# Three feed-forward layers: high weights meet high and low tokens in one 512-column up product, with ScalarE copying the low columns and VectorE adding the high ones

## The chip, the core and the metric

The program runs on one core of a Trainium2 chip. The metric is the device time in microseconds. The kernel before takes 1206.23 us, the median of three runs (1205.76, 1206.23 and 1207.28 us).

## What is computed

Two blocks follow each other on 256 tokens of width 1024. The first block is a gated linear attention mixer and a SwiGLU feed-forward layer (the FFN below). The second block has two layers, each a mixer and a squared-ReLU MLP. So there are three feed-forward layers:

```python
def swiglu(h, w_in, w_out):                 # the FFN: w_in 1024 x 5632, w_out 2816 x 1024
    gate, up = jnp.split(h @ w_in, 2, axis=-1)
    return (jax.nn.silu(gate) * up) @ w_out
...
for layer in range(DEPTH_2):                # two MLPs: mlp_w1 1024 x 4096, mlp_w2 4096 x 1024
    ...
    x = x + sq_relu_mlp(rms_norm_2(x, norm_mlp[layer]), mlp_w1[layer], mlp_w2[layer])
```

`sq_relu_mlp` squares the positive part of the up product, relu(xn @ w1)^2 @ w2. Everything is fp32.

## The kernel before

**Split products.** TensorE multiplies in the fp32r type, which keeps fewer bits than fp32. Each operand is therefore split in a high part, the value rounded to fp32r, and a low part, the rest. A product is three passes of TensorE that accumulate in one PSUM region (`split_mm`, L2105 to L2110): high by high (L2108), high by low (L2109) and low by high (L2110). The left factor of `split_mm` is the stationary one; it is loaded into the array before each pass, also where L2109 uses the same one as L2108. The high part of a weight tile is made by ScalarE (`high`, L687 to L690), the low part by VectorE (`low_weights`, L1169; it calls `low`, L1167).

**A feed-forward step.** The hidden width is worked off in steps: 128 gate and 128 up columns a step in the FFN (22 steps, numbered f = 0 to 21), 256 columns a step in an MLP (16 steps, twice). In one step of any of them the up product has 16 stationary weight tiles of 128x128 (8 tiles deep, times two halves: gate and up, or the two column halves). Each meets 256 tokens. The step's two halves land side by side in one PSUM bank, `bank[4 + j % 2]`. Then the hidden values are made and split:

- FFN: ScalarE writes silu(gate) from PSUM to `act_a` (L850). VectorE multiplies it with the up half in PSUM (L1473), casts the high part (L1474), and subtracts for the low part (L1167).
- MLP: ScalarE writes relu of both halves (512 columns) to `act_a` (L984). VectorE squares it (L1473), casts, subtracts.

The down product of the step has the hidden values as stationary operand and the down weights as moving one, 512 columns a pass: 12 passes in the FFN, 24 in an MLP, into banks 0 to 3.

**Order.** Each engine's queue is written out by hand, and semaphores tie them: `ff_ps` (up product done), `ff_act` (activation done), `ff_mid` (hidden values split), `w_used` (down product done), `loU_ready` and `loD_ready` (low part of the up and down weights ready), `hT_lo` (low part of the tokens ready, in four quarters). TensorE runs rounds of six steps in the FFN (rounds of four in an MLP): up(0), up(1), down(0), up(2), down(1), ..., up(5), down(4), down(5), then the next round. So within a round a down product has an up product between itself and the down product before it, and at a round's end two down products follow each other. The FFN's rounds end at f = 5, 11, 17 and 21. In each step ScalarE makes, after the activation, the high part of the up weights of two steps later and of the down weights of the next step, and VectorE makes the low parts after the hidden values. During the first round and a half of the FFN GpSimd sums slices of another weight matrix (`mod_sums`, L556 to L571).

## Time and profile before

| | |
|---|---|
| median of 3 runs | 1206.23 us |
| the profiled execution's own time | 1206.26 us |
| its span | 1204.5 us |
| TensorE busy | 1158.5 us (96%), 7472 matmuls |
| weight loads busy | 1005.1 us (83%) |
| VectorE busy | 741.7 us (62%), 1048 instructions |
| ScalarE busy | 556.6 us (46%), 760 instructions |
| GpSimd busy | 113.6 us (9%) |
| HBM traffic | 174 GB/s over the span |
| where they lie | FFN 233 to 421 us, MLPs 549 to 727 us and 1016 to 1195 us, about |

The busy time of an engine is the time in which at least one of its instructions is under way. Matmuls overlap: the duration of one is longer than the distance from its start to the next one's start. So what a pass costs is read from the starts, not from the durations. The ScalarE and VectorE rows give real durations. In a row of the timeline, brackets at the end hold the idle time before the instruction and what ended it.

### The profile page before, as it was taken

Reading aid. Unit: us, or ns where it says so; the run is one execution under the profiler, and the core shown is the slowest. Engines: PE = TensorE matmul, PEld = TensorE weight load, DVE = VectorE, ACT = ScalarE, POOL = GpSimd, SP = SyncE. Lnnn points to the kernel's source line nnn. Section 1 sums busy time; section 2 is a strip of 40 time slices with the busy share of each in tenths; the row PEclk is TensorE's granted clock in tenths of the full one; section 3 lists DMA queues with packets and bytes.
Section 4 is the critical chain, followed back from the end, with each engine's and each line's share of the span. In section 5 each row is a group of like instructions: output and inputs, shape, how many; then the busy total and the mean of one; then the engine's idle time right before and its main releaser. Section 6 shows DMA issues by size and latency. Waiting matters only on the chain.

```text
span 1204.5 us, 19086 instructions
## 1 busy us (share of the span) xinstructions
PE 1158.5 (96%) x7472; PEld 1005.1 (83%) x7476; DVE 741.7 (62%) x1048; ACT 556.6 (46%) x760; POOL 113.6 (9%) x109
## 2 busy tenths in 40 slices
PE   5899998899999989999999999999999999999997
PEld 2587775699999988648999999999999988999996
DVE  2887335697554586745465456776667776654653
ACT  3753232634333453644343346666666655433432
POOL 1000051187100070000000000000000000000000
PEclk9999999899999999999999999999999999999999
DMA  9674464977755540708554635555555434745500
GB/s 352 222 268 165 137 241 105 323 226 241 213 181 179 172 99 1 279 2 282 207 185 168 222 105 144 137 141 156 157 157 157 147 130 161 271 170 205 190 19 36
DMA packets 200241, 209.42 MB, mean 174 GB/s; under 512 B 6027, under 2 KB 167190, under 8 KB 199990
## 3 DMA queue, kind: packets, MB, share of 16 engines
q1 hardware_dynamic: 196480, 197.41, 51.3%
q0 software_dynamic: 2928, 9.02, 2.7%
q10 hardware_dynamic: 774, 2.17, 0.5%
q8 instruction: 40, 0.66, 0.2%
q14 instruction: 19, 0.16, 0.0%
HBM read 207.53 MB, written 2.01 MB: 174 GB/s over the span
## 4 chain that ended last, share of the span: by engine, by line
PE 90%; DVE 4%; ACT 2%; DMA 2%; issue 1%; ACTq 0%; DVEq 0%; SPq 0%
PE bank L2108 23%; PE bank L2110 23%; PE bank L2109 23%; PE bank L2378 2%; PE bank L1932 2%; PE bank L1934 2%; PE bank L1933 2%; PE bank L2505 1%; PE bank L2490 1%; PE bank L2481 1%; PE bank L2515 1%; DMA weight_pool<-in_gla_w_in_dram 1%; PE bank L1863 1%; DMA normed<-in_ctx_dram 1%; DMA weight_pool<-in_mod_w_dram 1%; PE bank L2361 1%
## 5 line engine op out<-in xcount | busy, mean ns | idle before, releaser
L2108 PE MATMUL bank<-hT_high,mlp_up_high 128*128 128x256 f32 x512 | 145.2, 284 | 0.9 <-DVE hT_low L1511 0.9
L2110 PE MATMUL bank<-hT_high,mlp_up_low 128*128 128x256 f32 x512 | 144.9, 283 | 0.0
L2109 PE MATMUL bank<-hT_low,mlp_up_high 128*128 128x256 f32 x512 | 144.9, 283 | 0.0
L2108 PE MATMUL bank<-od_w_high,hT_high 128*128 128x384 f32 x376 | 130.1, 346 | 0.0
L2110 PE MATMUL bank<-od_w_high,hT_low 128*128 128x384 f32 x376 | 126.1, 335 | 0.0
L2109 PE MATMUL bank<-od_w_low,hT_high 128*128 128x384 f32 x376 | 125.8, 334 | 0.0
L1167 DVE TENSOR_TENSOR mlp_down_low<-weight_pool,mlp_down_high 128x2048 fp32r<-128x2048 f32 x32 | 73.3, 2290 | 59.2 <-ACT mlp_down_high L690 59.2
L1167 DVE TENSOR_TENSOR od_w_low<-weight_pool,od_w_high 128x3072 fp32r<-128x3072 f32 x24 | 80.5, 3356 | 40.9 <-ACT od_w_high L690 40.9
L2108 PEld LDWEIGHTS bank<-hT_high,mlp_up_high 128*128 128x128 f32 x512 | 98.1, 192 | 2.8 <-issue 1.9
L2108 PE MATMUL bank<-hT_high,ffn_up_high 128*128 128x256 f32 x352 | 99.9, 284 | 0.0
L2108 PE MATMUL bank<-mlp_down_high,hidden_high 128*128 128x512 f32 x256 | 99.9, 390 | 0.0
L2109 PE MATMUL bank<-mlp_down_low,hidden_high 128*128 128x512 f32 x256 | 99.9, 390 | 0.0
L2110 PE MATMUL bank<-hT_high,ffn_up_low 128*128 128x256 f32 x352 | 99.6, 283 | 0.0
L2109 PE MATMUL bank<-hT_low,ffn_up_high 128*128 128x256 f32 x352 | 99.6, 283 | 0.0
L2110 PE MATMUL bank<-mlp_down_high,hidden_low 128*128 128x512 f32 x256 | 99.6, 389 | 0.0
L2109 PEld LDWEIGHTS bank<-hT_low,mlp_up_high 128*128 128x128 f32 x512 | 98.2, 192 | 0.9
L2110 PEld LDWEIGHTS bank<-hT_high,mlp_up_low 128*128 128x128 f32 x512 | 98.2, 192 | 0.0
L690 ACT ACTIVATE mlp_down_high<-weight_pool 128x2048 fp32r<-128x2048 f32 x32 | 61.2, 1912 | 71.0 <-PE bank L2110 71.0
L984 ACT ACTIVATE work<-bank 128x512 f32<-128x512 f32 x32 | 19.1, 598 | 137.6 <-PE bank L2110 137.6
L1473 DVE TENSOR_TENSOR work<-work 128x512 f32<-128x512 f32 x32 | 22.1, 690 | 89.4 <-ACT work L984 89.4
L1167 DVE TENSOR_TENSOR mlp_up_low<-weight_pool,mlp_up_high 128x2048 fp32r<-128x2048 f32 x32 | 73.2, 2289 | 2.6 <-ACT mlp_up_high L690 2.6
L2108 PEld LDWEIGHTS bank<-od_w_high,hT_high 128*128 128x128 f32 x376 | 70.6, 188 | 1.3 <-DVE od_w_low L1167 0.3
(367 smaller groups left out, 2697.7 us busy)
## 6 DMA issues: line engine op xcount, KB each, us to landing
weight_pool<-in_mlp_w_dram SPq DMA_DIRECT2D x64, 1024.0 KB, 7.8
weight_pool<-in_od_w_in_dram SPq DMA_DIRECT2D x72, 512.0 KB, 5.2
weight_pool<-in_ffn_w_in_dram SPq DMA_DIRECT2D x44, 512.0 KB, 5.7
weight_pool<-in_mod_w_dram SPq DMA_DIRECT2D x20, 1024.0 KB, 8.1
weight_pool<-in_gla_w_in_dram SPq DMA_DIRECT2D x12, 1024.0 KB, 8.3
weight_pool<-in_ffn_w_out_dram SPq DMA_DIRECT2D x22, 512.0 KB, 7.0
weight_pool<-in_gla_w_out_dram SPq DMA_DIRECT2D x2, 2048.0 KB, 14.2
normed<-in_mod_w_dram POOLq DMA_DIRECT2D x16, 256.0 KB, 5.1
```

The costliest lines, as they stand in the source:

```text
L690: act.activation(dst[:, :], pool[:, e.at + off:e.at + off + dst.shape[1]], ACT.Copy).then_inc(s[done], 1)
L984: act.activation(act_a[:, j % 2, :], bank[4 + j % 2][:, :], ACT.Relu).then_inc(s["ff_act"], 1)
L1167: dve.tensor_tensor(dst, whole, high.bitcast(F32), ALU.subtract).then_inc(s[done], 1)
L1473: chain(dve.tensor_tensor(whole, *product, ALU.mult))
L1863: ins = mm(slice_bank(i, 0)[lo:lo + 32, :], silc[:, k, :], slice_weights(i, k), start=(k < 4), stop=(k >= 4))
L1932: mm(out_, left[0], right[0], start=start, stop=False)
L1933: mm(out_, left[0], right[1], start=False, stop=False)
L1934: return mm(out_, left[1], right[0], start=False, stop=stop)
L2108: mm(out_, left[0], right[0], start=start, stop=False, **flag)
L2109: mm(out_, left[0], right[1], start=False, stop=False, **flag)
L2110: return mm(out_, left[1], right[0], start=False, stop=stop, **flag)
L2378: ins = mm(bank[b][:, :], oT[:, k, P * t:P * t + P], pv(e)[:, k % 4, 512 * (b % 2):512 * (b % 2) + 512], start=(k == 4), stop=(k == 3))
```

## The change

The tokens' high and low parts lie one after the other in `hT`, and a strided view of both, `hT_both[:, k]`, is 512 columns in two pieces of 256. The up product of a weight tile is now two passes in place of three: the high weights meet all 512 columns, and the low weights meet the 256 high ones, which accumulate on the first half. So a half of a step fills a whole PSUM bank: columns 0 to 255 hold high by high plus low by high, columns 256 to 511 hold high by low, and the two halves of the bank have still to be added. A step has two banks, and banks 4 to 7 serve two steps.

ScalarE copies the two low halves to `act_a` (`low_products`), and VectorE adds the high halves from PSUM (`sum_halves`). In the FFN ScalarE then waits for the first sum (`ff_sum`) and takes the silu of it in SBUF. In an MLP the relu is folded into VectorE's square. The first step of the FFN takes another order of its tiles and no longer starts with a pass that zeroes a bank; step 19 waits for columns that use banks 6 and 7.

```diff
+        hT_halves = over("hT_halves", "hT", 0, 4096)
+        hT2 = [view(hT_halves, 2048 * i, KD, SEQ) for i in range(2)]
+        hT_both = hT_halves[:, :].rearrange("p (w k t) -> p k w t", w=2, k=KD)
+        def up_bank(j, part):
+            return bank[4 + 2 * (j % 2) + part]
...
# ScalarE
+            def low_products(j):
+                for part in range(2):
+                    ins = act.activation(act_a[:, j % 2, 256 * part:256 * part + 256], up_bank(j, part)[:, 256:512], ACT.Copy)
+                ins.then_inc(s["ff_act"], 1)
...
-                act.activation(act_a[:, j % 2, 0:256], bank[4 + j % 2][:, 0:256], ACT.Silu).then_inc(s["ff_act"], 1)
+                low_products(j)
+                act.wait_ge(s["ff_sum"], f + 1)
+                act.activation(act_a[:, j % 2, 0:256], act_a[:, j % 2, 0:256], ACT.Silu).then_inc(s["ff_act"], 1)
...
-                    act.activation(act_a[:, j % 2, :], bank[4 + j % 2][:, :], ACT.Relu).then_inc(s["ff_act"], 1)
+                    low_products(j)
...
# VectorE
+            def sum_halves(j, part):
+                v = act_a[:, j % 2, 256 * part:256 * part + 256]
+                return dve.tensor_tensor(v, v, up_bank(j, part)[:, 0:256], ALU.add)
...
-                dve.wait_ge(s["ff_act"], f + 1)
+                dve.wait_ge(s["ff_act"], 2 * f + 1)
+                sum_halves(j, 0).then_inc(s["ff_sum"], 1)
+                chain(sum_halves(j, 1))
+                dve.wait_ge(s["ff_act"], 2 * f + 2)
...
-                split_hidden(j, 256, (act_a[:, j % 2, 0:256], bank[4 + j % 2][:, 256:512]))
+                split_hidden(j, 256, lambda whole: dve.tensor_tensor(whole, act_a[:, j % 2, 0:256], act_a[:, j % 2, 256:512], ALU.mult))
...
-                    split_hidden(j, 512, (act_a[:, j % 2, :], act_a[:, j % 2, :]))
+                    both_sums = act_a[:, j % 2, :]
+                    split_hidden(j, 512, lambda whole: dve.scalar_tensor_tensor(out=whole, in0=both_sums, scalar=0.0, in1=both_sums,
+                                                                                op0=ALU.max, op1=ALU.mult))
...
# TensorE
+            def up_mm(out_, w, k, n):
+                mm(out_[:, :], w[0], hT_both[:, k], start=(n == 0), stop=False, skip_group_check=True)
+                return mm(out_[:, 0:256], w[1], hT2[0][:, k, :], start=False, stop=(n == KD - 1), skip_group_check=True)
...
+                if isinstance(f, int) and f == FF_LOOPS * FF_RING + 1:
+                    pe.wait_ge(s["mod_cols"], 12)
-                    if first and n == 0 and g == 0:
-                        mm(bank[4][:, :], zero[:, 0:P], zero[:, :], start=True, stop=False, skip_group_check=True)
...
-                            ins = split_mm(bank[4 + j % 2][:, 256 * f:256 * f + 256],
-                                           both(mlU[j % 2], lambda x: x[:, 256 * k + P * f:256 * k + P * f + P]),
-                                           both(hT2, lambda x: x[:, k, :]), n == 0, n == KD - 1)
+                            ins = up_mm(up_bank(j, f), both(mlU[j % 2], lambda x: x[:, 256 * k + P * f:256 * k + P * f + P]), k, n)
```

The order on ScalarE at the first two FFN steps; `work` is where `act_a` lies. Before:

```order
L690 ACTIVATE ffn_up_high<-weight_pool 128x2048 [waits w_ffn1,out_used]
L850 ACT_TABLE_LOAD
L850 ACTIVATE work<-bank 128x256 [waits ff_ps]
L690 ACTIVATE ffn_up_high<-weight_pool 128x2048 [waits w_ffn2]
L690 ACTIVATE ffn_down_high<-weight_pool 128x1024 [waits w_ffn1]
L850 ACTIVATE work<-bank 128x256 [waits ff_ps]
```

Now:

```order
L697 ACTIVATE ffn_up_high<-weight_pool 128x2048 [waits w_ffn1,out_used]
L856 ACTIVATE work<-bank 128x256 [waits ff_ps]
L856 ACTIVATE work<-bank 128x256
L865 ACT_TABLE_LOAD
L865 ACTIVATE work<-work 128x256 [waits ff_sum]
L697 ACTIVATE ffn_up_high<-weight_pool 128x2048 [waits w_ffn2]
L697 ACTIVATE ffn_down_high<-weight_pool 128x1024 [waits w_ffn1]
L856 ACTIVATE work<-bank 128x256 [waits ff_ps]
```

The silu, which stood first and waited for TensorE alone, now stands behind two copies and waits for VectorE's first sum; the weight parts behind it stand where they stood. The load of silu's table moved behind the copies of the first step.

VectorE from the second up weights' low part to the second step. Before:

```order
L1167 TENSOR_TENSOR ffn_up_low<-weight_pool,ffn_up_high 128x2048 [waits hiU_ready]
L1473 TENSOR_TENSOR work<-work,bank 128x256 [waits ff_act]
L1474 CAST hidden_high<-work 128x256 [waits dve_chain]
L1167 TENSOR_TENSOR hidden_low<-work,hidden_high 128x256 [waits dve_chain]
L1167 TENSOR_TENSOR ffn_up_low<-weight_pool,ffn_up_high 128x2048 [waits hiU_ready]
L1167 TENSOR_TENSOR ffn_down_low<-weight_pool,ffn_down_high 128x1024 [waits hiD_ready]
L1473 TENSOR_TENSOR work<-work,bank 128x256 [waits ff_act]
```

Now:

```order
L1182 TENSOR_TENSOR ffn_up_low<-weight_pool,ffn_up_high 128x2048 [waits hiU_ready]
L1488 TENSOR_TENSOR work<-work,bank 128x256 [waits ff_act]
L1488 TENSOR_TENSOR work<-work,bank 128x256
L1504 TENSOR_TENSOR work<-work 128x256 [waits ff_act,dve_chain]
L1494 CAST hidden_high<-work 128x256 [waits dve_chain]
L1182 TENSOR_TENSOR hidden_low<-work,hidden_high 128x256 [waits dve_chain]
L1182 TENSOR_TENSOR ffn_up_low<-weight_pool,ffn_up_high 128x2048 [waits hiU_ready]
L1182 TENSOR_TENSOR ffn_down_low<-weight_pool,ffn_down_high 128x1024 [waits hiD_ready]
L1488 TENSOR_TENSOR work<-work,bank 128x256 [waits ff_act]
```

Two additions that read PSUM came in ahead of the product, and the product itself now reads two operands in SBUF (`work<-work`), where it read one in PSUM (`work<-work,bank`).

TensorE at the start of the FFN's second round, up(6). Before:

```order
L2108 MATMUL bank<-hT_high,ffn_up_high 128x256 [waits hT_lo,ff_mid]
L2109 MATMUL bank<-hT_low,ffn_up_high 128x256
L2110 MATMUL bank<-hT_high,ffn_up_low 128x256
L2108 MATMUL bank<-hT_high,ffn_up_high 128x256
L2109 MATMUL bank<-hT_low,ffn_up_high 128x256
```

Now:

```order
L2184 MATMUL bank<-hT_halves,ffn_up_high 128x512 [waits hT_lo,ff_mid]
L2185 MATMUL bank<-hT_halves,ffn_up_low 128x256
L2184 MATMUL bank<-hT_halves,ffn_up_high 128x512
L2185 MATMUL bank<-hT_halves,ffn_up_low 128x256
L2184 MATMUL bank<-hT_halves,ffn_up_high 128x512 [waits hT_lo]
```

Three passes of 256 columns with three loads became one of 512 and one of 256 with two loads; the waits are the same.

## Rows read from the trace of the kernel before

**Rows 1.** the page: the chain that ended last, its shares by engine
```profile
PE 90%; DVE 4%; ACT 2%; DMA 2%; issue 1%; ACTq 0%; DVEq 0%; SPq 0%
```

**Rows 2.** windows, 300 to 350 us: busy us of each engine (instructions), granted clock, DMA share, GB/s
```profile
300.00:350.00 50.00, 50.00 (x354) 47.08 (x353) 29.39 (x31) 18.80 (x18) 6.14 (x4) 1.00 0.63 191
```

**Rows 3.** timeline, TensorE, a feed-forward step of the MLP: start us, duration us
```profile
599.79 0.28 PE L2108 MATMUL bank<-hT_high,mlp_up_high 128*128 128x256 f32 x1
...
605.55 0.40 PE L2108 MATMUL bank<-mlp_down_high,hidden_high 128*128 128x512 f32 x1
...
607.17 0.39 PE L2109 MATMUL bank<-mlp_down_low,hidden_high 128*128 128x512 f32 x1
...
611.02 0.28 PE L2108 MATMUL bank<-hT_high,mlp_up_high 128*128 128x256 f32 x1
...
611.25 0.28 PE L2110 MATMUL bank<-hT_high,mlp_up_low 128*128 128x256 f32 x1
```

**Rows 4.** timeline, TensorE, odd mixer's projection: 384 columns in three pieces
```profile
765.88 0.33 PE L2108 MATMUL bank<-od_w_high,hT_high 128*128 128x384 f32 x1
...
766.75 0.34 PE L2110 MATMUL bank<-od_w_high,hT_low 128*128 128x384 f32 x1
```

**Rows 5.** groups by form: busy us, mean ns of one, idle before
```profile
L2108 PE MATMUL bank<-hT_high,mlp_up_high 128*128 128x256 f32 x512 | 145.2, 284 | 0.9 <-DVE hT_low L1511 0.9
...
L2108 PE MATMUL bank<-hT_high,ffn_up_high 128*128 128x256 f32 x352 | 99.9, 284 | 0.0
...
L1551 DVE TENSOR_TENSOR work<-work 128x256 f32<-128x256 f32 x48 | 20.4, 425 | 1.6
```

**Rows 6.** timeline, ScalarE, end of the FFN
```profile
416.55 0.38 ACT L850 ACTIVATE work<-bank 128x256 f32<-128x256 f32 x1 [4.69 <-PE bank L2110]
416.83 1.59 ACT L690 ACTIVATE ev_c_high<-weight_pool 128x1664 fp32r<-128x1664 f32 x1
```

**Rows 7.** timeline, VectorE, end of the FFN
```profile
416.97 0.42 DVE L1473 TENSOR_TENSOR work<-work,bank 128x256 f32<-128x256 f32 x1 [3.85 <-ACT work L850]
417.43 0.29 DVE L1474 CAST hidden_high<-work 128x256 fp32r<-128x256 f32 x1
417.75 0.43 DVE L1167 TENSOR_TENSOR hidden_low<-work,hidden_high 128x256 fp32r<-128x256 f32 x1
```

**Rows 8.** timeline, TensorE, one down product of the FFN, and the next up product
```profile
304.10 0.40 PE L2108 MATMUL bank<-ffn_down_high,hidden_high 128*128 128x512 f32 x1
...
306.85 0.28 PE L2108 MATMUL bank<-hT_high,ffn_up_high 128*128 128x256 f32 x1
```

**Rows 9.** timeline, ScalarE, silu of the FFN's first and ninth step
```profile
239.06 0.38 ACT L850 ACTIVATE work<-bank 128x256 f32<-128x256 f32 x1 [2.60 <-PE bank L2110]
...
304.30 0.38 ACT L850 ACTIVATE work<-bank 128x256 f32<-128x256 f32 x1 [4.69 <-PE bank L2110]
```

**Rows 10.** timeline, VectorE, first round of the FFN: start, duration, idle before
```profile
236.27 2.28 DVE L1167 TENSOR_TENSOR ffn_up_low<-weight_pool,ffn_up_high 128x2048 fp32r<-128x2048 f32 x1
...
254.62 0.41 DVE L1473 TENSOR_TENSOR work<-work,bank 128x256 f32<-128x256 f32 x1
...
255.79 1.47 DVE L1167 TENSOR_TENSOR hidden_low<-work,hidden_high 128x256 fp32r<-128x256 f32 x1
...
262.24 0.42 DVE L1473 TENSOR_TENSOR work<-work,bank 128x256 f32<-128x256 f32 x1 [0.79 <-ACT work L850]
...
270.74 0.42 DVE L1473 TENSOR_TENSOR work<-work,bank 128x256 f32<-128x256 f32 x1 [1.47 <-ACT work L850]
...
279.24 0.42 DVE L1473 TENSOR_TENSOR work<-work,bank 128x256 f32<-128x256 f32 x1 [2.47 <-ACT work L850]
```

**Rows 11.** timeline, GpSimd in the same stretch
```profile
255.69 1.29 POOL L571 TENSOR_TENSOR normed<-normed 128x512 f32<-128x512 f32 x1
```

**Rows 12.** timeline, ScalarE, end of the first MLP
```profile
717.91 0.60 ACT L984 ACTIVATE work<-bank 128x512 f32<-128x512 f32 x1 [3.84 <-PE bank L2110]
```

**Rows 13.** timeline, VectorE, end of the first MLP
```profile
718.54 0.69 DVE L1473 TENSOR_TENSOR work<-work 128x512 f32<-128x512 f32 x1 [2.14 <-ACT work L984]
```

More of the change, by code:

```diff
@@ L1489, in _ @@
             with dve.Fori(0, FF_LOOPS - 1) as i:
-                chain.enter(i, 2 * FF_RING)
+                chain.enter(i, 3 * FF_RING)
                 for j in range(FF_RING):
@@ L2171, in ffn_up @@
                         pe.wait_ge(s["hT_lo"], n // 2 + 1)
-                    if first and n == 0 and g == 0:
-                        mm(bank[4][:, :], zero[:, 0:P], zero[:, :], start=True, stop=False, skip_group_check=True)
-                    ins = split_mm(bank[4 + j % 2][:, 256 * g:256 * g + 256],
-                                   both(ffU[j % 2], lambda x: x[:, 1024 * g + P * k:1024 * g + P * k + P]),
-                                   both(hT2, lambda x: x[:, k, :]), n == 0 and not first, n == KD - 1, running=first)
+                    ins = up_mm(up_bank(j, g), both(ffU[j % 2], lambda x: x[:, 1024 * g + P * k:1024 * g + P * k + P]), k, n)
                 ins.then_inc(s["ff_ps"], 1)
```

16 lines of the change are left out of this document (9 added, 7 removed).

## The prediction

> **What bounds the kernel now.** I read the chain of waits first. TensorE holds 90% of it [rows 1]: what shortens TensorE's own work in a feed-forward layer shortens the kernel, and work on the other engines counts only where TensorE comes to wait for it. The windows say the same of a stretch inside the FFN: TensorE is busy in 50.00 of 50 us, VectorE in 29.39 and ScalarE in 18.80, at a granted clock of 1.00, which is the 2.4 GHz level [rows 2].
>
> Then the timeline of TensorE, because the durations mislead. A 256-column pass has a mean duration of 284 ns [rows 5], but the 48 passes of one up product start between 599.79 and 605.55, so one costs 5.76 / 48 = 0.120 us. The down product behind it runs to 611.02; its last 17 passes, from 607.17 on, take 3.85 us or 0.2265 us each [rows 3]. The odd mixer's 384-column passes start 0.87 us apart over five, 0.174 us each [rows 4]. At 2.4 GHz the columns alone are 0.1067, 0.2133 and 0.160 us. Each size leaves the same remainder, 0.0133 us (0.014 for 384): what a pass costs is its columns plus about 13.3 ns, whatever their number, with one weight load a pass.
>
> **The passes, the gain.** The change leaves the number of columns as it is, 768 for a weight tile, and takes one pass and one load away: 3 x 0.120 = 0.360 us becomes 0.2267 + 0.120 = 0.3467 us. There are 352 tiles in the FFN and 512 in the MLPs [rows 5], 864 together, so 864 x 0.0133 = 11.5 us. I take this value. The moving operand now lies in two pieces; rows 4 has three pieces at the same remainder, so I cost this at nothing.
>
> No row shows 512 and 256 columns in turn for long, so the bounds come from where the two sizes meet. The first seven 512-column passes after a row of 256-column ones take 605.55 to 607.17, 1.62 us, against 7 x 0.2265 = 1.585; and the first two 256-column passes afterwards take 0.23 us, against 0.24 [rows 3]. So a change of sizes up costs about 0.03 us spread over some passes, and one down gives 0.01 back. The best case is that an alternating stream keeps what it gains: 13.3 + 1.7 ns, 13 us together. The worst is that every tile pays the 20 ns of a full round trip, which is a loss of 6.7 ns, -5.8 us together. In between, each 512-column pass is at 0.234 and each 256-column one at 0.120: 6 ns a tile, 5.2 us. I stay at 13.3, since a shift of a few ns in the start of a pass that is given back by the next is what the 0.01 looks like.
>
> The Trainium skill ("TensorE: Matmul & The Clock Gate", "Wait — 56ns, not 53.3ns?") puts the fixed cost of a warm pass at about 2.5 ns, and its "Step-by-step: what each phase is for" says that the next tile's weights load behind the running matmul; by these two, 864 passes fewer would be worth only 2.2 us. Rows 3 and 4 have 13.3 ns over the columns at three sizes, so here the trace disagrees, and the sum goes by the trace.
>
> **The hidden values, where nothing is lost.** Inside a round, TensorE has a down and an up product between the end of up(f) and down(f), 2.75 [rows 8] + 16 x 0.3467 = 8.3 us in the FFN. Even in an MLP at a round's end there is the whole down product, 605.55 to 611.02 = 5.47 us [rows 3]. In an MLP the relu of 0.60 us [rows 12] becomes two copies of 256 columns, 0.28 + 0.38 = 0.66 us [rows 6], then two additions of 0.42 [rows 7], then the square at 0.69 [rows 13], and cast and low part as before. I put the new square, which takes a maximum too, at the same 0.69; the chain grows by some 1.0 us and was about 2.7 us with its cast and low part (which I estimate from the FFN's at twice the columns). 3.7 us fit into 5.47, so both MLPs lose nothing; with additions twice as slow they still fit. VectorE's added 0.9 us a step are idle time now, in MLP and FFN alike (20 of 50 us in rows 2).
>
> The first step of the FFN loses its zeroing pass. That gains nothing: up(1) needs the low part of the second weights, which is ready at 236.27 + 2.28 = 238.55 [rows 10], and the first silu at 239.06, 0.2 us after up(0)'s end [rows 9], says that up(1) started at 238.86. Between them lie 0.3 us, which the 16 shorter tiles already use up. The silu's table load, now behind the copies, falls into the 5.5 us of up(1). Step 19's new wait on the mod columns stands a whole up product after they are asked for: nothing.
>
> **The hidden values at a round's end in the FFN, the loss.** Here only one down product of 2.75 us [rows 8] stands before down(f), at f = 5, 11, 17 and 21. The silu starts 0.20 us after that down product (304.30 against 304.10) [rows 8, 9]. At the end of the FFN this gives a down product from 416.35 to 419.10, and the low part was ready at 417.75 + 0.43 = 418.18 [rows 7]: 0.9 us to spare. Now, on the same time scale: copies 416.55 and 416.83, done 417.21; first sum 417.25 to 417.67; silu from SBUF at the same 0.38, 417.71 to 418.09, with the second sum beside it; product 418.13; cast 0.46 later, low part another 0.32 later and 0.43 long, done 419.34 [rows 6, 7]. That is 0.24 us too late, and with the release of TensorE about 0.4 us. Three round ends without GpSimd at work, f = 11, 17, 21: 1.2 us.
>
> The end at f = 5 is worse. While GpSimd runs [rows 11], VectorE's operations with two SBUF operands stretch: hidden_low of 256 columns took 1.47 us [rows 10], against 0.43 when alone [rows 7]. VectorE was behind in the first steps (no idle time before the product at 254.62), and from 262.24 to 279.24 it caught up, with 0.79, 1.47 and 2.47 us of idle time before its products [rows 10], 4.7 us in all. The change adds 0.9 us to each of about five steps and shortens each by 0.21, 5.6 us together, so that it has no spare time left and comes about 1 us late to f = 5. With the 0.4 us of the chain I take 1.5 us. The bounds are 0.4 (no lag) and 4 (each product stretched to 1.4 us as well, over three or four steps). The product that read PSUM kept 0.41 and 0.42 us in this stretch [rows 10], and it now reads two SBUF operands (the sibling with two SBUF operands takes 425 ns alone [rows 5]). The Trainium skill ("SBUF — State Buffer", "The single rule") says why that matters: the pair of ports that VectorE and GpSimd share is an exclusive lock, taken by a VectorE operation with two SBUF inputs. The 1.47 us beside GpSimd's 1.29 us operation at 255.69 [rows 11] agree.
>
> **The sum.** Made against the profiled execution: 1206.26 us, of which the span is 1204.5; this execution stands 0.03 us over the median. 1206.26 - 11.5 + 1.2 + 1.5 = 1197.5 us.
>
> **The rivals.**
> Size changes cost more than a load: 20 ns a tile, as in the round trip of rows 3. Then -13.3 turns to +6.7 ns, and with the 2.7 us of the round ends the time is 1206.3 + 5.8 + 2.7 = 1214.8. It decides from 13.3 ns a switch on. For it speaks that rows 3 do have a transient; against it that it dies out within seven passes of the same size and is given back in part. Chance 0.08.
> Half of it: 0.234 and 0.120, 1206.3 - 5.2 + 2.7 = 1203.8, on the edge of what can be told. Chance 0.08.
> The load is hidden and the 13.3 ns belong to each 256 columns written rather than to a pass: nothing is gained by the merge, and the 2.7 us of loss put the time at 1208.9; if the pass itself still frees some of it, it is less. Three equal remainders at three sizes [rows 3, 4] speak against it. Chance 0.05, on the edge between same and slower. With the 2.5 ns of the Trainium skill ("TensorE: Matmul & The Clock Gate", section named above) it would be 1206.8.
> VectorE falls behind further in the first round, the 4 us of the bound, and the other round ends cost 0.8 instead of 0.4 us: 1206.3 - 11.5 + 4 + 2.4 = 1201.2. The ports speak for it, and against it that GpSimd is busy for only 6.14 us after 300 us [rows 2], f = 8. Chance 0.10.
> More gain: 15 ns a tile and round ends that fit after all: 1206.3 - 13 + 0.6 = 1193.9. Chance 0.07.
> The rest, 0.62, is the forecast, 1195 to 1200.5.
>
> **Range and chances.** A measurement of this kernel can tell about 0.2%, 2.4 us, from no change; so faster means under 1203.8. Faster: forecast, more gain, the slow VectorE, and half of the half case: 0.83. Same: the other half and most of the 0.05 of the hidden load, 0.08. Slower: 0.09, with the rest of it. The range runs from 1194.0 to 1203.5: it leaves out most of the gain's case and the two bad ones.
>
> **What would show it.** Starts of TensorE inside an up product: a pair of 512 and 256 columns every 0.347 us right, 0.354 half, 0.367 wrong. The MLP step, 11.2 us in before (48 x 0.120 and 5.47), at 11.0. The idle time of TensorE before down(11), down(17) and down(21) at 0.4 us each, with VectorE's hidden_low as releaser, and 1 to 2 us before down(5); none before any down product of an MLP. VectorE's product in the first round at more than 0.42 us in places. The forecast is wrong if the pair takes over 0.354 us, or if TensorE waits inside rounds.

## The result, and the profile after

| | before | after |
|---|---|---|
| median of 14 runs each, us | 1206.39 | 1209.11 |
| lowest to highest, us | 1205.64 to 1207.64 | 1206.77 to 1212.16 |
| profiled execution: time, span, us | 1206.26, 1204.5 | 1208.3, 1206.5 |
| TensorE, first product of the FFN to that of the first MLP, us | 316.20 | 322.06 |
| first MLP's first product to the second's, us | 466.67 | 464.92 |
| second MLP's first product to the last pass, us | 179.42 | 177.63 |

The ratio is 1.0021 (95% interval 1.0013 to 1.0029): slower by 0.2%, where 1197.5 us and a gain were forecast. The last three lines, read from TensorE's timelines, say where. Both MLPs gained, 1.75 and 1.79 us, close to 16 steps x 0.112 us = 1.79. The FFN lost 5.86 us. The first of these lines runs on beyond the last down product, to the first MLP. All accounts below are those of the profiled execution, which is 0.8 us under the median; the times of after scatter over 5.4 us, those of before over 2.0.

The page's first and fourth parts, of the kernel after:

```profile
PE 1156.9 (96%) x6611; PEld 960.3 (80%) x6611; DVE 783.7 (65%) x1156; ACT 572.3 (47%) x836; POOL 110.3 (9%) x109
...
PE 72%; DVE 3%; ACT 1%; issue 0%; DVEq 0%; ACTq 0%
```

TensorE's share of the chain went from 90 to 72% [rows 1]. The busy shares hardly tell anything; the stretch of the FFN does.

Groups by line, of after (busy us, mean ns of one, idle before):

```profile
L2184 PE MATMUL bank<-hT_halves,mlp_up_high 128*128 128x512 f32 x512 | 181.9, 398 | 0.9 <-DVE hT_halves L1534 0.9
L2185 PE MATMUL bank<-hT_halves,mlp_up_low 128*128 128x256 f32 x512 | 143.7, 281 | 0.0
```

As in [rows 5] the mean duration misleads, and the starts count. Timeline of TensorE, after, one up product of the first MLP (start us, duration us):

```profile
599.39 0.40 PE L2184 MATMUL bank<-hT_halves,mlp_up_high 128*128 128x512 f32 x1
599.62 0.28 PE L2185 MATMUL bank<-hT_halves,mlp_up_low 128*128 128x256 f32 x1
599.74 0.40 PE L2184 MATMUL bank<-hT_halves,mlp_up_high 128*128 128x512 f32 x1
599.98 0.28 PE L2185 MATMUL bank<-hT_halves,mlp_up_low 128*128 128x256 f32 x1
600.10 0.40 PE L2184 MATMUL bank<-hT_halves,mlp_up_high 128*128 128x512 f32 x1
```

Unrounded, the starts stand 227, 113 and then 233, 117, 241, 120, 236, 113 ns apart, and these six come again and again: three pairs in 1060 ns, 353.3 a pair. With its start the whole up product takes 5.640 us for 16 pairs, 352.5 ns each (before 5.752 us), not 346.7. Against the 359.5 of before (5.752 / 16) that is 7.0 ns a tile, and 54 steps x 0.112 = 6.05 us in all instead of 11.5.

Not every stretch is like this. The second step of the same MLP has the same instructions in the same order:

```profile
560.37 0.39 PE L2184 MATMUL bank<-hT_halves,mlp_up_high 128*128 128x512 f32 x1
560.60 0.28 PE L2185 MATMUL bank<-hT_halves,mlp_up_low 128*128 128x256 f32 x1
560.71 0.39 PE L2184 MATMUL bank<-hT_halves,mlp_up_high 128*128 128x512 f32 x1
```

Here the starts stand 230 and 117 ns apart all the way, 346.7 ns a pair, and the up product takes 5.546 us: the number of the prediction. After runs at this pace in the FFN's first two steps (234.3 to 244.0) and around the second step of both MLPs (557.6 to 565.6 and 1022.5 to 1030.5), and at the slower one in nearly all the rest.

The FFN's first round, windows of after (busy us of TensorE, its loads, VectorE, ScalarE, GpSimd, then granted clock, DMA share, GB/s):

```profile
232.00:256.00 24.00, 23.20 (x119) 19.34 (x119) 21.12 (x22) 12.49 (x17) 16.61 (x14) 0.96 0.70 211
256.00:279.00 23.00, 23.00 (x123) 19.37 (x122) 22.17 (x22) 10.83 (x13) 15.80 (x15) 1.00 0.77 246
279.00:291.00 12.00, 8.48 (x34) 6.63 (x34) 10.82 (x9) 3.82 (x5) 9.03 (x7) 0.86 0.81 267
```

and of before:

```profile
256.00:279.00 23.00, 23.00 (x171) 21.98 (x170) 17.99 (x13) 7.75 (x8) 16.45 (x15) 1.00 0.87 276
279.00:291.00 12.00, 12.00 (x82) 11.09 (x81) 6.96 (x6) 3.94 (x5) 10.82 (x10) 1.00 0.78 234
```

VectorE had 5.0 us to spare between 256 and 279 us and has 0.8 now. Then TensorE is busy in only 8.48 of 12 us, at a mean clock of 0.86. Its timeline there, down(5):

```profile
281.82 0.39 PE L2137 MATMUL bank<-ffn_down_high,hidden_low 128*128 128x512 f32 x1
285.73 0.80 PE L2135 MATMUL bank<-ffn_down_high,hidden_high 128*128 128x512 f32 x1 [3.52 <-DVE hidden_low L1182]
286.32 0.63 PE L2136 MATMUL bank<-ffn_down_low,hidden_high 128*128 128x512 f32 x1
286.75 0.63 PE L2137 MATMUL bank<-ffn_down_high,hidden_low 128*128 128x512 f32 x1
...
288.45 0.49 PE L2135 MATMUL bank<-ffn_down_high,hidden_high 128*128 128x512 f32 x1
288.78 0.39 PE L2136 MATMUL bank<-ffn_down_low,hidden_high 128*128 128x512 f32 x1
```

Two passes start 3.91 us apart that should start 0.23 apart: a wait of 3.68 us. Behind it the passes start 0.427 us apart instead of 0.227, up to 288.5: the granted clock is at 1.2 GHz from 285.2 to 288.6. With the slow restart of the first passes that costs another 1.46 us.

Why VectorE was late, its timeline in after (the products and what surrounds them; idle before in brackets):

```profile
239.70 0.75 DVE L1488 TENSOR_TENSOR work<-work,bank 128x256 f32<-128x256 f32 x2 [1.44 <-ACT work L856]
241.50 1.27 DVE L1504 TENSOR_TENSOR work<-work 128x256 f32<-128x256 f32 x1 [1.04 <-ACT work L865]
...
243.13 1.59 DVE L1182 TENSOR_TENSOR hidden_low<-work,hidden_high 128x256 fp32r<-128x256 f32 x1
244.64 3.37 DVE L1182 TENSOR_TENSOR ffn_up_low<-weight_pool,ffn_up_high 128x2048 fp32r<-128x2048 f32 x1
247.94 2.06 DVE L1182 TENSOR_TENSOR ffn_down_low<-weight_pool,ffn_down_high 128x1024 fp32r<-128x1024 f32 x1
249.92 0.74 DVE L1488 TENSOR_TENSOR work<-work,bank 128x256 f32<-128x256 f32 x2
...
259.14 1.27 DVE L1494 CAST hidden_high<-work 128x256 fp32r<-128x256 f32 x1
...
282.25 0.74 DVE L1488 TENSOR_TENSOR work<-work,bank 128x256 f32<-128x256 f32 x2
283.19 0.54 DVE L1504 TENSOR_TENSOR work<-work 128x256 f32<-128x256 f32 x1 [0.21 <-DVE work L1488]
283.76 0.29 DVE L1494 CAST hidden_high<-work 128x256 fp32r<-128x256 f32 x1
284.09 1.58 DVE L1182 TENSOR_TENSOR hidden_low<-work,hidden_high 128x256 fp32r<-128x256 f32 x1
```

and ScalarE's, after:

```profile
244.56 0.66 ACT L856 ACTIVATE work<-bank 128x256 f32<-128x256 f32 x2 [0.41 <-PE bank L2185]
250.36 0.42 ACT L865 ACTIVATE work<-work 128x256 f32<-128x256 f32 x1 [5.14 <-DVE work L1488]
...
279.50 0.66 ACT L856 ACTIVATE work<-bank 128x256 f32<-128x256 f32 x2 [1.69 <-PE bank L2185]
```

In step 0 the copies end and the additions follow at once. In step 1 the copies are done at 245.22 and the additions start at 249.92, a lag of 4.7 us: the four stretched operations of the rows between took 1.27, 1.59, 3.37 and 2.06 us, where the same four take 0.43, 0.42, 2.31 and 1.22 us without GpSimd (run e3_gpsimd_idle), 3.9 us more. A lag of 1.3 us is there at this place in that run too, behind the table load of step 0, and is gone one step later. From step to step the lag is then 4.7, 3.1, 3.2, 2.4 and 2.1 us: it is being paid back, since VectorE needs 8.1 us a step (249.92 to 282.25 over four) and TensorE 8.4, but too slowly. Inside the round a down and an up product hide it. Before down(5) nothing does, and the wait is the sum of known parts: lag 2.1, hidden_low 1.58 instead of 0.43, product 0.54 instead of 0.42, and the 0.36 of a round end without GpSimd: 3.7 us.

The FFN's account: the passes give 22 x 0.112 = 2.46 us, the stretch is 5.86 us longer, so 8.3 us are lost. Down(5): 3.68 + 1.46 (clock and slow restart) = 5.1. Down(11), (17) and (21): 0.47 to 0.49 each, 1.4. Small new waits, each with its slow restart, before down(0) 0.5, up(2) 0.6 and up(3) 0.2: 1.3. The rest is 0.5. Some 0.3 of it lies in up(0) and up(1), which take 6.35 and, without the wait, 5.55 us (6.08 and 5.76 before): the clock was at half until 234.0 us, 1.6 us after the first product instead of 0.3. The other 0.2 has no place of its own; no run was made for this rest.

### The profile page after: what moved, and what is told of

Same layout as the page of the kernel before. It is cut to its first block, busy times and chain, and to the rows that moved or that the text cites. A ratio compares the mean times of both kernels' runs of the same rounds, so it can differ in the third digit from the quotient of the medians.

```text
span 1206.5 us, 17623 instructions
## 1 busy us (share of the span) xinstructions
PE 1156.9 (96%) x6611; PEld 960.3 (80%) x6611; DVE 783.7 (65%) x1156; ACT 572.3 (47%) x836; POOL 110.3 (9%) x109
## 4 chain that ended last, share of the span: by engine, by line
PE 72%; DVE 3%; ACT 1%; issue 0%; DVEq 0%; ACTq 0%
PE bank L2184 15%; PE bank L2135 13%; PE bank L2137 13%; PE bank L2136 13%; PE bank L2185 8%; PE bank L2409 2%; PE bank L2534 1%; PE bank L2519 1%; PE bank L2510 1%; PE bank L2544 1%; PE bank L2392 1%; PE bank L2148 1%; PE bank L2369 1%; PE bank L2525 1%; PE bank L2379 1%; PE bank L1877 0%
## 5 line engine op out<-in xcount | busy, mean ns | idle before, releaser
L2184 PE MATMUL bank<-hT_halves,mlp_up_high 128*128 128x512 f32 x512 | 181.9, 398 | 0.9 <-DVE hT_halves L1534 0.9
L2185 PE MATMUL bank<-hT_halves,mlp_up_low 128*128 128x256 f32 x512 | 143.7, 281 | 0.0
L2135 PE MATMUL bank<-od_w_high,hT_halves 128*128 128x384 f32 x376 | 130.1, 346 | 0.0
L2184 PE MATMUL bank<-hT_halves,ffn_up_high 128*128 128x512 f32 x352 | 125.9, 400 | 0.5 <-DVE ffn_up_low L1182 0.3
L2137 PE MATMUL bank<-od_w_high,hT_halves 128*128 128x384 f32 x376 | 126.1, 335 | 0.0
L2136 PE MATMUL bank<-od_w_low,hT_halves 128*128 128x384 f32 x376 | 125.8, 335 | 0.0
L2184 PEld LDWEIGHTS bank<-hT_halves,mlp_up_high 128*128 128x128 f32 x512 | 96.1, 188 | 25.6 <-issue 1.9
L2185 PE MATMUL bank<-hT_halves,ffn_up_low 128*128 128x256 f32 x352 | 99.1, 281 | 0.0
L2185 PEld LDWEIGHTS bank<-hT_halves,mlp_up_low 128*128 128x128 f32 x512 | 96.7, 189 | 0.9
L2135 PEld LDWEIGHTS bank<-od_w_high,hT_halves 128*128 128x128 f32 x376 | 70.6, 188 | 1.3 <-DVE od_w_low L1182 0.3
L2136 PEld LDWEIGHTS bank<-od_w_low,hT_halves 128*128 128x128 f32 x376 | 70.7, 188 | 0.0
L2137 PEld LDWEIGHTS bank<-od_w_high,hT_halves 128*128 128x128 f32 x376 | 70.5, 188 | 0.0
```

Of the source, the lines that this page charges most:

```text
L2135: mm(out_, left[0], right[0], start=start, stop=False, **flag)
L2136: mm(out_, left[0], right[1], start=False, stop=False, **flag)
L2137: return mm(out_, left[1], right[0], start=False, stop=stop, **flag)
L2184: mm(out_[:, :], w[0], hT_both[:, k], start=(n == 0), stop=False, skip_group_check=True)
L2185: return mm(out_[:, 0:256], w[1], hT2[0][:, k, :], start=False, stop=(n == KD - 1), skip_group_check=True)
```

## Experiments

Each result is set against runs of the kernel before on the same chip in the same stretch (medians 1206.31 to 1206.56). The three stretches of the profiled executions, us:

| run | median us | ratio (95%) | FFN | MLP to MLP | to the end |
|---|---|---|---|---|---|
| before | | 1 | 316.20 | 466.67 | 179.42 |
| after | 1209.11 | 1.0021 (1.0013 to 1.0029) | 322.06 | 464.92 | 177.63 |
| e1_mlp_only | 1202.45 | 0.9968 (0.9956 to 0.9980) | 315.84 | 464.89 | 177.63 |
| e2_grouped | 1207.78 | 1.0007 (0.9998 to 1.0017) | 323.34 | 464.50 | 177.23 |
| e3_gpsimd_idle | 1202.92 | 0.9973 (0.9963 to 0.9982) | 315.50 | 465.10 | 177.81 |
| e4_sum_in_bank | 1207.97 | 1.0009 (1.0000 to 1.0019) | 322.44 | 465.10 | 177.81 |
| e5_mlp_only_grouped | 1203.12 | 0.9970 (0.9957 to 0.9982) | 317.92 | 464.51 | 177.20 |
| e6_groups_of_two | 1206.64 (one) | none | 322.98 | 463.54 | 176.29 |
| e9_no_adds | 1200.81 | 0.9950 (0.9935 to 0.9965) | 313.76 | 464.91 | 177.81 |
| e10_continuous | 1204.54 | 0.9986 (0.9977 to 0.9996) | 316.91 | 464.90 | 177.64 |
| e11_continuous_twos | 1199.29 | 0.9935 (0.9918 to 0.9951) | 316.54 | 463.55 | 176.30 |
| e12_mlp_only_twos | 1200.30 | 0.9948 (0.9932 to 0.9965) | 315.87 | 463.58 | 176.28 |
| e13_paced_continuous_twos | 1196.97 | 0.9920 (0.9903 to 0.9936) | 312.87 | 463.55 | 176.28 |
| e14_paced | 1202.71 | 0.9966 (0.9954 to 0.9979) | 315.74 | 464.90 | 177.81 |

**e1_mlp_only.** The FFN as before, both MLPs as in after.

```diff
-                low_products(j)
-                act.wait_ge(s["ff_sum"], f + 1)
-                act.activation(act_a[:, j % 2, 0:256], act_a[:, j % 2, 0:256], ACT.Silu)
+                act.activation(act_a[:, j % 2, 0:256], bank[4 + j % 2][:, 0:256], ACT.Silu)
...
-                sum_halves(j, 0).then_inc(s["ff_sum"], 1)
-                chain(sum_halves(j, 1))
...
-                    ins = up_mm(up_bank(j, g), ...)
+                    ins = split_mm(bank[4 + j % 2][:, 256 * g:256 * g + 256], ...)
```

> The FFN as in the kernel before, the two MLPs with the merged up product. If the loss lies in the FFN's first round alone (theory), the MLPs keep what their 32 up products show in the trace of after, 5.64 instead of 5.752 us each: 32 x 0.112 = 3.6 us less than before, 1202.8 us, and no wait of TensorE before any down product. Rival, that something of the loss is spread over all three layers (a longer start of the MLPs, a lower clock): 1204.5 us or more.

Measured 1202.45 us. TensorE waits before no down product of an MLP, and its up products take 5.640 us there and 5.752 in the FFN. So the loss of after is in the FFN alone, 6.7 us between the two kernels (of which the profiles' FFN stretches show 6.2).

**e3_gpsimd_idle.** After, with GpSimd's products and additions on 8 of their 512 columns.

```diff
-g.tensor_tensor(w if k else sum_row(i), w, factor, ALU.mult)
+n8 = 8 if k else 512
+g.tensor_tensor((w if k else sum_row(i))[:, 0:n8], w[:, 0:n8], silc[:, k, 0:1].to_broadcast([P, n8]), ALU.mult)
...
-g.tensor_tensor(sum_row(i), sum_row(i), w, ALU.add)
+g.tensor_tensor(sum_row(i)[:, 0:8], sum_row(i)[:, 0:8], w[:, 0:8], ALU.add)
```

> The changed kernel, in which GpSimd's products and additions during the FFN's first round work on 8 of 512 columns (so the sums of two slices of the modulation weights are left out; its DMAs and signals stay). Theory, that VectorE is slowed by sharing its ports with GpSimd: VectorE's step in the first round falls from 8.3 us to about 6.4, TensorE's wait before down(5) from 3.5 to 0.4 us, the clock does not drop behind it, the waits before down(0) and up(2) go: 6 to 7 us less than after, about 1202.5 us. Rival, that the new chain (two copies, sum, silu, product) is what makes VectorE late: a wait of 3 us before down(5) stays, 1208 us or more.

Measured 1202.92 us. VectorE's timeline at the first round's end, e3_gpsimd_idle:

```profile
279.14 0.75 DVE L1489 TENSOR_TENSOR work<-work,bank 128x256 f32<-128x256 f32 x2 [2.24 <-ACT work L857]
280.10 0.43 DVE L1505 TENSOR_TENSOR work<-work 128x256 f32<-128x256 f32 x1 [0.21 <-DVE work L1489]
280.56 0.29 DVE L1495 CAST hidden_high<-work 128x256 fp32r<-128x256 f32 x1
280.89 0.43 DVE L1183 TENSOR_TENSOR hidden_low<-work,hidden_high 128x256 fp32r<-128x256 f32 x1
```

VectorE is idle for 2.24 us before the additions, nothing is stretched, and the two passes around the wait before down(5) start 0.601 us apart, a wait of 0.37. No clock drop, no wait before down(0) or up(2). GpSimd's load on VectorE is worth 6.2 us to this kernel, of which down(5) is 3.3 for the wait and 1.4 for the clock.

**e9_no_adds.** After, but silu and product read the banks directly; the part of gate and up that comes of high weights and low tokens stays out of the hidden values.

```diff
-                low_products(j)
-                act.wait_ge(s["ff_sum"], f + 1)
-                act.activation(act_a[:, j % 2, 0:256], act_a[:, j % 2, 0:256], ACT.Silu)
+                act.activation(act_a[:, j % 2, 0:256], up_bank(j, 0)[:, 0:256], ACT.Silu)
...
-                sum_halves(j, 0).then_inc(s["ff_sum"], 1)
-                chain(sum_halves(j, 1))
```

> The merged up product in all three layers, but in the FFN no copies and no additions: silu and product read the banks directly as before (so the high-by-low part of the FFN's gate and up values is left out), while GpSimd works as in the kernel before. Theory, that VectorE's and ScalarE's added work in the first round is what turns into TensorE's waits: no wait before down(0) to down(5) nor at later round ends, 54 x 0.112 = 6.0 us less than before, 1200.4 us. Rival, that the faster TensorE alone overtakes VectorE beside GpSimd: waits of 1 us or more before down(5) stay.

Measured 1200.81 us, and no wait before any down product. The FFN stretch is 313.76 us; 316.20 - 2.46 = 313.74. So TensorE's side of the change in the FFN is worth its passes and nothing else, and what after loses hangs on the copies and additions and on the silu's and product's wait for them.

**e4_sum_in_bank.** The second sum stays in PSUM, so that the product reads one operand there, as before.

```diff
-return dve.tensor_tensor(v, v, up_bank(j, part)[:, 0:256], ALU.add)
+v, b = act_a[:, j % 2, 256 * part:256 * part + 256], up_bank(j, part)[:, 0:256]
+return dve.tensor_tensor(b if in_bank else v, v, b, ALU.add)
...
+chain(sum_halves(j, 1, in_bank=True))
...
-... act_a[:, j % 2, 0:256], act_a[:, j % 2, 256:512], ALU.mult))
+... act_a[:, j % 2, 0:256], up_bank(j, 1)[:, 0:256], ALU.mult))
```

> The changed kernel, with VectorE's second addition in the FFN written back to the PSUM bank, so that the product reads one operand in PSUM as before. Theory, that the product's second SBUF operand let GpSimd's lock in: the product keeps 0.42 us in all six steps of the first round (in after up to 1.27, 1.1 us in all), VectorE is 1.1 us earlier at f = 5, and so is the end of TensorE's wait, about 1208 us. Rival, that the stretching moves on to the cast and hidden_low behind it: the product at 0.42, the wait before down(5) at 3.5 us as it was, 1209.1 us.

Measured 1207.97 us. VectorE's timeline, e4_sum_in_bank:

```profile
249.59 0.42 DVE L1504 TENSOR_TENSOR work<-work,bank 128x256 f32<-128x256 f32 x1 [0.21 <-ACT work L865]
250.05 1.09 DVE L1494 CAST hidden_high<-work 128x256 fp32r<-128x256 f32 x1
...
282.09 0.42 DVE L1504 TENSOR_TENSOR work<-work,bank 128x256 f32<-128x256 f32 x1 [0.20 <-DVE bank L1488]
282.54 0.29 DVE L1494 CAST hidden_high<-work 128x256 fp32r<-128x256 f32 x1
282.87 1.70 DVE L1182 TENSOR_TENSOR hidden_low<-work,hidden_high 128x256 fp32r<-128x256 f32 x1
```

The product takes 0.42 us in all six steps, but in each one the operation behind it takes the stretch: the cast 1.09 or 1.10 in three, hidden_low 1.15 to 1.70 in the others. The wait before down(5) is 4.0 us (passes 4.25 apart). The time agreed with the number that I gave my theory (but the 1.1 us to after lie within the scatter of both), the trace with the rival: what the product gains is lost one operation later, so the product's second SBUF operand isn't the cause.

**e10_continuous.** Down(5), (11) and (17) stand behind the next round's first up product.

```diff
                 for j in range(n):
                     ffn_up(f0 + j, j)
-                    if j:
-                        ffn_down(f0 + (j - 1), j - 1)
-                ffn_down(f0 + (n - 1), n - 1, last)
+                    if j or not first:
+                        ffn_down(f0 + (j - 1), (j - 1) % FF_RING)
...
+            ffn_down(FFC - 1, (FFC - 1) % FF_RING, True)
```

> The changed kernel, with TensorE's order in the FFN changed at the round ends: down(5), down(11) and down(17) stand behind the next round's first up product, like every other down product. Theory, that a lag of VectorE of some 3.5 us matters only where one down product of 2.75 us covers the hidden values: with 8.4 us of cover the wait before down(5), the clock's drop behind it (1.8 us) and the two 0.47 us waits go, up to 1 us comes back at the columns of step 18, about 1203.5 us. Rival, that VectorE beside GpSimd is too slow at every step: the wait only moves to the next products, 1206 us or more.

Measured 1204.54 us (1203.26 to 1206.52). No long wait and no clock drop are left; the waits at round ends are gone but for the last. Now TensorE meets the late VectorE in small pieces, 0.1 to 0.35 us before each of the seven up products that stand behind a down product from 246.6 to 298.9 us: it has caught up with it. Another 0.6 us come at 393.4, before the up product of step 19, where after has no wait of TensorE. The FFN takes 316.91 us, 0.7 more than before. Cover at the round end is worth 5.2 us of the FFN stretch; VectorE's load still costs the passes' gain.

**e14_paced.** After, with GpSimd's units spread: each waits until TensorE has used one more weight chunk.

```diff
                     g.wait_ge(s[f"sums_in{n % 2}"], 16 * (n // 2) + 16)
+                    if n:
+                        g.wait_ge(s["w_used"], n)
```

> The changed kernel with nothing but GpSimd paced, one unit a step. If the wait of 3.7 us before down(5) and the clock's drop behind it come from the density of GpSimd's work: a wait of 0.4 us there as at the other round ends, no drop, about 6 us less than the changed kernel and close to the run with GpSimd idle (1202.9): 1203.3 us. Rival, that any GpSimd work in a step costs VectorE the same: the wait stays at 2 us or more and comes at the later round ends too, 1208 us or more.

Measured 1202.71 us, 6.4 less than after for a wait on an engine that nothing waits for. Windows, e14_paced:

```profile
232.00:256.00 24.00, 23.33 (x124) 19.38 (x123) 20.64 (x29) 14.55 (x20) 6.71 (x7) 1.00 0.72 219
256.00:279.00 23.00, 23.00 (x124) 19.70 (x123) 18.70 (x17) 9.93 (x14) 14.47 (x9) 1.00 0.73 228
279.00:291.00 12.00, 11.79 (x61) 9.67 (x60) 7.14 (x8) 4.07 (x6) 7.78 (x6) 1.00 0.73 227
```

GpSimd is busy for 6.7 instead of 16.6 us up to 256, and VectorE, which has done 29 operations there instead of 22, comes out of the first steps without a lag. The wait before down(5) is 0.37 us, as at the other round ends (0.36), and the clock stays up. GpSimd still does all of its work.

**e2_grouped.** After, but in each half of an up product the eight 512-column passes stand first and the eight 256-column ones behind them (the FFN's first step as in after).

```diff
+            def up_group(out_, weights, ns, before=lambda n: None):
+                for n in ns:
+                    before(n)
+                    mm(out_[:, :], weights(K_ORDER[n])[0], hT_both[:, K_ORDER[n]], ...)
+                for n in ns:
+                    ins = mm(out_[:, 0:256], weights(K_ORDER[n])[1], hT2[0][:, K_ORDER[n], :], ...)
```

> The changed kernel with the same passes in another order: in each half of a step first the 8 passes of 512 columns, then the 8 of 256 (all steps but the FFN's first). Theory, that the missing 6 ns a pair are the price of changing the size: the up product takes 16 x 0.3467 plus one transient, 5.57 us instead of 5.64, and the kernel 53 x 0.07 = 3.7 us less than after, 1205.4 us. Rival, that a 512-column pass whose moving operand lies in two pieces costs 240 ns by itself: up product at 5.64 us, kernel at 1209.1 us.

Measured 1207.78 us. The up product takes 5.559 us, 347.4 ns a pair against the 346.7 that I had worked out for a pass with its load at 13.3 ns over its columns: the gain that I predicted is there in every step inside a round of an MLP when passes of one size stand together. Two things took it back. The wait before down(5) was 4.0 us, with 6.8 us at half clock behind it. And the first step of each MLP lost 1.0 us, TensorE's timeline, e2_grouped:

```profile
555.87 3.00 PE L2191 MATMUL bank<-hT_halves,mlp_up_high 128*128 128x512 f32 x8 [0.55 <-DVE hT_halves L1534]
558.70 1.12 PE L2193 MATMUL bank<-hT_halves,mlp_up_low 128*128 128x256 f32 x8
```

Eight 512-column passes take 2.83 us here and not 1.81, because hT's low parts arrive in pairs and the 256-column passes, which need none, no longer fill the time.

**e5_mlp_only_grouped.** e1 with the groups of e2 in the MLPs.

```diff
-                    ins = up_mm(up_bank(j, f), ...)
+                    for n0 in range(0, KD, 8):
+                        ins = up_group(up_bank(j, f), ..., range(n0, n0 + 8), arrived)
```

> The FFN as before; in the two MLPs the merged up product with the passes grouped (8 of 512 columns, then 8 of 256 in each half of a step). From e1 (1202.45 us) and the grouped up product of e2 (5.56 in place of 5.64 us): 32 x 0.08 = 2.6 us less, 1199.9 us; 0.5 us of it may go at the first step of each MLP, where the 512-column passes run ahead of the tokens' low parts. Rival, that grouping costs elsewhere: 1202 us or more.

Measured 1203.12 us, a miss. The MLPs' first steps lost 1.0 us each as in e2. And the FFN, which is that of before, took 317.92 us in the profiled execution: TensorE's timeline, e5_mlp_only_grouped:

```profile
283.09 0.50 PE L2130 MATMUL bank<-ffn_down_high,hidden_high 128*128 128x512 f32 x1 [1.19 <-DVE hidden_low L1180]
```

So the first round end stood near its edge already before the change: the same FFN waits there in one execution and not in another. VectorE had no lag here, it was idle for 2.60 us before the product (2.47 in before); what made it late is that both operations behind the product met GpSimd, the cast with 1.50 us (0.47 in before) and hidden_low with 1.44 (0.43). No clock drop follows this wait.

**e6_groups_of_two.** Groups of two 512-column and two 256-column passes (a single run, so no interval).

```diff
-                        for n0 in range(0, KD, 8):
+                        for n0 in range(0, KD, 2):
```

> The changed kernel with the passes in groups of two (two of 512 columns, two of 256). What is read is the length of an up product inside a round: 5.64 us in turn and 5.56 in groups of eight. If each round trip between the sizes costs the same, about 6 ns, it is 16 x 0.3467 + 8 x 0.006 = 5.595 us. If the cost is that of the transient between up and down products, 20 ns for each round trip that is long enough to show it, it is 5.70 us.

Neither number came: the up product takes 5.563 us, 347.7 ns a pair, as much as in groups of eight. Every second change of size is gone, but nearly the whole of the 5 ns is. So the cost isn't one per change of size. It doesn't belong to single passes in turn as such either, since after has stretches of them at 346.7 ns. Which pace they take differs between executions of the same instructions: the second step of the second MLP takes 5.547 us in after, e1 and e10 and 5.650 in e3, e4, e9 and e14, and this is why the last column of the table has 177.63 in three runs and 177.81 in four. In groups of two an up product inside a round takes 5.563 us in each MLP of each run that has them. The first MLP step loses nothing now. TensorE's timeline, e6_groups_of_two:

```profile
599.96 0.62 PE L2191 MATMUL bank<-hT_halves,mlp_up_high 128*128 128x512 f32 x2
600.41 0.40 PE L2193 MATMUL bank<-hT_halves,mlp_up_low 128*128 128x256 f32 x2
600.64 0.63 PE L2191 MATMUL bank<-hT_halves,mlp_up_high 128*128 128x512 f32 x2
601.11 0.39 PE L2193 MATMUL bank<-hT_halves,mlp_up_low 128*128 128x256 f32 x2
```

A group of four passes takes 0.69 us. The two MLP stretches are 463.54 and 176.29 us, 3.1 and 3.1 us under before; by the up product it is 359.5 - 347.7 = 11.8 ns a tile. The FFN waited before down(5) as in e2.

**e12_mlp_only_twos.** e1 with groups of two in the MLPs.

```diff
-                    for n0 in range(0, KD, 8):
+                    for n0 in range(0, KD, 2):
```

> The FFN as before, the MLPs with the merged product in groups of two. From 1202.45 us of the MLPs alone in turn: 32 x 0.077 = 2.5 us less, and no wait in the first step of an MLP, since only two passes run ahead of the tokens' low parts: 1200.0 us. If the FFN as it was makes TensorE wait before down(5) in some executions (1.3 us in the profile of the groups of eight), up to 1201.3.

Measured 1200.30 us: 3.1 + 3.1 us of it are the MLPs', as the profile shows, and 6.1 the difference of the medians.

**e11_continuous_twos.** e10 with groups of two in all three layers.

```diff
-                    if j:
+                    if j or not first:
...
-                            ins = up_mm(up_bank(j, f), ...)
+                        for n0 in range(0, KD, 2):
+                            ins = up_group(up_bank(j, f), ...)
```

> The changed kernel with two mends: TensorE's order without the round ends in the FFN (as the run before, 1204.5 us) and the passes in groups of two in all three layers (up product 5.563 in place of 5.64 us). If TensorE bounds all but the FFN's first steps, 54 x 0.077 = 4.2 us less, less about 0.7 us for some nine steps in which VectorE sets the pace whatever TensorE does: 1201.0 us. Rival, that VectorE sets the pace in the whole FFN: only the MLPs' 32 x 0.077 = 2.5 us, 1202.0 us.

Measured 1199.29 us (1198.18 to 1201.23), under the expected 1201.0. The profiled execution was the slowest of the four, and its FFN, 316.54 us, holds 3.4 us at half clock from 394.5 on, with no long wait ahead of it. That drop I can't explain from the trace.

**e13_paced_continuous_twos.** e11 with e14's pacing.

```diff
+                    if n:
+                        g.wait_ge(s["w_used"], n)
```

> All three layers merged, groups of two, no round ends, and GpSimd paced: it does one of its 16 units a step (each waits for one more down product), where it did 1.8. VectorE's step then is 6.4 us of its own and about 1.05 of stretching, under the 8.3 us of TensorE's step, so no wait is left in the first steps. From the kernel before: 54 x (0.112 + 0.077) = 10.2 us less, 0.5 back at the FFN's end and 0.3 around step 18: 1197 us. Rival, that each unit of GpSimd stretches VectorE by its whole 2.3 us: 8.7 us a step, waits of 0.4 us in some 16 steps, 1202 us or more.

Measured 1196.97 us (1196.40 to 1198.08), 0.8% under before: it beats both kernels. The FFN takes 312.87 us; 316.20 - 22 x 0.189 leaves 312.0, the rest is 0.8, for which the trace has the last round end with 0.5 and a wait of 0.6 at 390.0, before the up product of step 19, together somewhat more than that. TensorE is busy in all of 256 to 291 us. GpSimd's work now reaches beyond 300 us (26.2 us busy from 300 to 350, where 5.8 were), and no wait of TensorE follows from it.

## Why the prediction was wrong

**The passes, the gain: the step was mis-sized.** I had 13.3 ns a tile and 11.5 us; measured are 7.0 ns and 6.05 us. The remainder of 13.3 ns for a pass with its load was right (e2: 347.4 ns a pair), and the two-piece operand cost nothing, as I put it. What failed is the choice within my own bounds: "I stay at 13.3", with the transient of [rows 3] read as something that is given back. In nearly all steps it isn't: 352.5 ns a pair, near the 0.354 us of the rival "half of it", to which I gave 0.08. But the stretches of after at 346.7 ns show that the same passes in turn can keep the whole gain, and by e6 next to nothing is paid per change of size. So there are two paces for one sequence of instructions, and what sets the pace stays open.

The Trainium skill's figure of 2.5 ns for a warm pass ("TensorE: Matmul & The Clock Gate", "Wait — 56ns, not 53.3ns?") doesn't hold for these fp32r passes, each with its own load: a pass and a load less brought 7.0 ns in turn and 11.8 ns in groups of two.

**The end at f = 5: the step that made it slower.** I had 1.5 us with a bound of 4; it cost 5.1, and the whole first round with its small waits and its start some 6.9. The sign that I had named for a wrong forecast, TensorE waiting inside rounds, came before down(0), up(2) and up(3). Three parts were missing. First, the lag: I took VectorE's spare time of before over five steps against the work added over five steps, and got 1 us. But in the first step the table load cost VectorE some time and four operations beside GpSimd took 3.9 us longer, so that the lag began at 4.7 us, and a VectorE with no idle time left paid back 2.6 of it in four steps; 2.1 were left. I should have followed the lag, not the balance of a stretch. Second, the chain of down(5) itself: I counted it at its lengths without GpSimd, though [rows 10] had hidden_low at 1.47; e5 shows that this part alone can cost 1.35 us, even with the FFN of before. Third, the clock: after 3.5 us without a pass TensorE came back at 1.2 GHz, 1.4 us, which I hadn't in any of my cases. E3 and e14 take the load off VectorE in two ways and get 6.2 and 6.4 us back; e9 and e10 agree.

**The product with two SBUF operands.** It took 1.27, 0.55, 0.42, 0.43, 0.42 and 0.54 us: stretched in places, as foreseen, but e4 shows that this isn't what decides. The Trainium skill ("SBUF — State Buffer", "Who interferes with whom") has the shared ports as an exclusive lock, which a VectorE operation with two SBUF inputs can meet and a cast in a 2-port mode too. The trace agrees in that both kinds are stretched, the cast of 0.29 us to 1.27, while in e4 the product with an operand in PSUM kept 0.42 us in all six steps; the mode of the cast no row shows. The rule tells which operation may wait; that another one behind it will wait in its place is what I missed.

**The other round ends, right.** 0.47, 0.47 and 0.49 us against 0.4, with VectorE's hidden_low as releaser. That they were cheap is also why GpSimd's part in f = 5 is clear: the same chain, without it.

**The MLPs, right.** No wait before a down product of either. The table load behind the first copies (239.69 to 240.97) cost TensorE nothing by itself, as I had put it: in e3 and e14 it stands in the same place, and no wait before down(0) follows.

**The sum with what was measured.** 1206.26 - 6.05 + 5.1 (f = 5) + 1.4 (three round ends) + 1.3 (small waits) + 0.5 (first products) = 1208.5, against 1208.3. The 0.5 is the FFN's remainder, so the FFN's part of this sum fits by construction; what it tells is the sizes. Half the gain was missing and the loss was three times too small. My rivals had each of them, at 0.08 and 0.10, but only one at a time: both together were needed to end on the other side, and VectorE beside GpSimd was the one I should have drawn as the rival that does so.

## What to carry to other kernels

When work is moved onto an engine that is idle on average, follow its lag step by step from the first step on, with each operation at its length beside its neighbour, and look for the place in the order where the cover is least. A background engine that nobody waits for may still set the time through a shared resource; pacing it over the stretch cost nothing here and brought 6.4 us. Passes of two sizes were better put in twos than in turn: 5.563 us an up product, where in turn it was 5.640 in most steps and 5.547 in a few, and which of the two could not be foreseen. In eights it was as good inside, but the first step lost 1.0 us, because its inputs arrive in pairs.

## What was not expected of the hardware

- Passes of 512 and 256 columns, one of each in turn, run at one of two paces: 353.3 ns a pair, with starts that repeat after three pairs (233, 117, 241, 120, 236, 113 ns), or 346.7 (in after 230, 117). The same instructions take the one in some runs and the other in others (second step of the second MLP). In twos a pair costs 347.7 ns, in eights 347.4, in every step inside a round of an MLP.
- At 1.2 GHz a 512-column pass takes 426.5 ns, its columns and no remainder; at 2.4 GHz 226.5 for 213.3. The 13.3 ns are there only at the high clock.
- Waits of TensorE of 3.7 to 4.1 us before down(5) each had a stretch at 1.2 GHz behind them, which began before the wait's end (3.4 us in after, 6.8 in e2, e4 and e6); one of 1.35 us (e5) had none. One such stretch has no long wait ahead of it (e11, at 394.5 us).
- Beside GpSimd operations of 1.3 us, VectorE's take about 1.1 us longer when they meet one: the cast 1.27 for 0.29, hidden_low 1.58 for 0.43, the 2048-column part 3.4 to 3.6 for 2.3. It goes both ways: GpSimd's operations of 1.05 and 1.3 us take 2.1 to 3.2 in places, as at 262.29 (3.22), beside VectorE's 2048-column part (the profile's spans of GpSimd are rough).
